# A hybrid decoder layer on one core: another fixed order of the steps where one unit of sparse attention ends and the next begins

## The reference

```python
z = rms_norm(x) @ w_in
# per group of 4 heads that share keys and values
p_cmp = masked_softmax(q . k_cmp);   o_cmp = p_cmp @ v_cmp
imp = sum over the 4 heads of p_cmp @ overlap      # importance of blocks of 64 keys
sel = top_k(imp + forced blocks, 8)
o_slc = softmax(q . k_s over the selected blocks, causal) @ v_s
o_win = softmax(q . k_w over the last 256 keys) @ v_w
o = gate0 * o_cmp + gate1 * o_slc + gate2 * o_win
x = x + concat(retention, short conv, o) @ w_out
x = x + relu(rms_norm(x) @ w_up) ** 2 @ w_down
```

## Time and profile before

| | us |
|---|---|
| median of 3 runs | 3399.78 |
| lowest, highest | 3397.82, 3400.06 |
| the profiled execution, device time | 3393.48 |
| its span, first to last instruction | 3391.7 |
| projection, about | 593 |
| mixers, first to last TensorE instruction | 593 to 1712 |
| output projection and MLP | 1712 to 3392 |

### The profile page before, as it was taken

One profiled execution on the slowest core, in us unless ns is written; L12 is line 12 of the kernel. 1 busy time (PEld: TensorE's weight loads), 2 busy tenths in 40 slices (PEclk: granted clock), 3 DMA queues, 4 the chain that ended last, 5 costly groups with the idle time before them and its releaser, 6 DMA issues. The chain is left out here.

```text
span 3391.7 us, 42938 instructions
## 1 busy us (share of the span) xinstructions
PE 3179.0 (94%) x15498; PEld 2487.8 (73%) x15498; DVE 1443.5 (43%) x2633; ACT 1003.8 (30%) x1660; POOL 1065.3 (31%) x607
## 2 busy tenths in 40 slices
PE   7999998778889999999989699999999999999999
PEld 7999998654555555555458578888888878888887
DVE  3113111456565666665422233345333643354333
ACT  3012000334444444444321132233223222232221
POOL 3212220424232422221010144444444444444442
PEclk9999999678899999999989889999999999999999
DMA  5233221201010100010033332224222332223221
GB/s 175 98 110 100 99 96 63 94 27 65 33 65 33 65 33 33 33 39 7 7 143 134 137 125 94 95 91 149 99 91 95 119 117 98 89 85 124 99 99 62
DMA packets 160807, 289.88 MB, mean 85 GB/s; under 512 B 15023, under 2 KB 122415, under 8 KB 158636
## 3 DMA queue, kind: packets, MB, share of 16 engines
q1 hardware_dynamic: 150908, 270.00, 23.2%
q10 hardware_dynamic: 9776, 18.24, 1.6%
HBM read 237.68 MB, written 50.53 MB: 85 GB/s over the span
## 5 line engine op out<-in xcount | busy, mean ns | idle before, releaser
L1792 POOL TENSOR_TENSOR mlp_down_lo<-mlp_down_raw,mlp_down_hi 128x2048 fp32r<-128x2048 f32 x64 | 298.4, 4663 | 747.7 <-ACT mlp_down_hi L1831 747.7
L1912 DVE TENSOR_TENSOR mlp_y<-mlp_acc,mlp_y 128x512 f32<-128x512 f32 x512 | 344.4, 688 | 198.3 <-PE mlp_acc L1990 194.0
L1990 PE MATMUL mlp_acc<-mlp_down_hi,mlp_f_hi 128*128 128x512 f32 x1024 | 401.2, 392 | 10.5 <-DVE mlp_y L1912 10.5
L1968 PE MATMUL mlp_up<-mlp_hT_hi,mlp_up_hi 128*128 128x512 f32 x1024 | 399.4, 390 | 2.5 <-DVE mlp_hT_lo L1934 2.5
L1990 PE MATMUL mlp_acc<-mlp_down_hi,mlp_f_lo 128*128 128x512 f32 x1024 | 399.3, 390 | 0.0
L1968 PE MATMUL mlp_up<-mlp_hT_hi,mlp_up_lo 128*128 128x512 f32 x1024 | 399.1, 390 | 0.0
L1990 PE MATMUL mlp_acc<-mlp_down_lo,mlp_f_hi 128*128 128x512 f32 x1024 | 399.1, 390 | 0.0
L1968 PE MATMUL mlp_up<-mlp_hT_lo,mlp_up_hi 128*128 128x512 f32 x1024 | 399.1, 390 | 0.0
L1899 DVE TENSOR_TENSOR mlp_f<-mlp_relu 128x512 f32<-128x512 f32 x128 | 134.3, 1050 | 602.1 <-ACT mlp_relu L1838 602.1
L328 PE MATMUL proj_acc<-proj_w_hi,proj_hT_hi 128*128 128x344 f32 x1152 | 370.2, 321 | 10.0 <-issue 9.4
L328 PE MATMUL proj_acc<-proj_w_hi,proj_hT_lo 128*128 128x344 f32 x1152 | 368.3, 320 | 0.0
(11 more groups left out here) (259 smaller groups left out, 5377.6 us busy)
## 6 DMA issues: line engine op xcount, KB each, us to landing
mlp_up_raw<-in_w_up SPq DMA_DIRECT2D x64, 1024.0 KB, 5.2
mlp_down_raw<-in_w_down SPq DMA_DIRECT2D x64, 1024.0 KB, 4.8
proj_w_raw<-in_w_in SPq DMA_DIRECT2D x18, 1376.0 KB, 6.3
z_scratch<-proj_z_out SPq DMA_DIRECT2D x144, 172.0 KB, 1.8
mix_z<-z_scratch SPq DMA_DIRECT2D x16, 1548.0 KB, 6.9
proj_x_tile<-in_x ACTq DMA_DIRECT2D x16, 512.0 KB, 4.0
mixed_scratch<-mix_mixed SPq DMA_DIRECT2D x16, 512.0 KB, 3.0
out_mixed<-mixed_scratch SPq DMA_DIRECT2D x16, 512.0 KB, 4.1
```

The costliest lines, as they stand in the source:

```text
L1792: nc.gpsimd.tensor_tensor(dn_lo[:, b, :, :], dn_raw[:, :, :], dn_hi[:, b, :, :].bitcast(F32), ALU.subtract).then_inc(dn_lo_done, 1)
L1912: nc.vector.tensor_tensor(y[:, yb, tt, cols], acc[i % AR][:, :], y[:, yb, tt, cols], ALU.add).then_inc(added, 1)
L1968: mm = nc.tensor.matmul(up_ps[t % 2][:, :], w[:, b, k, cols], h[:, k, :], start=k == 0 and w is up_hi and h is h_hi, stop=k == KT - 1 and ...
L1990: mm = nc.tensor.matmul(acc[i % AR][:, :], a[:, b, k, tt * P:(tt + 1) * P], w[:, b, k, c * BANK:(c + 1) * BANK], start=k == 0 and a is f_h ...
```

## The change

The rules of `Plan` are rewritten where a unit ends. No instruction is added or dropped, no semaphore and no buffer is changed; the list has the same 2019 steps. Three things are different:

1. The window's lift, turn and post (`front_end`) leave `front`, the selected branch's last values and lift leave `own`, and `row` is split from the selected maxima. They are written out in a head: row, window lift, last values, selected lift, window turn, first scores, window post, selected turn, second scores, select, selected, selected post.
2. What is merged in the body of a unit is shorter by those steps, so the prep pieces, which are spread by count, lie closer together and end earlier; the row stands last in it.
3. The merge is nested in another way: maxima with front and prep first, then own.

```diff
--- before.py
+++ after.py
@@ -468,10 +468,11 @@
 
     def __init__(self, tiles):
         units = tiles * GROUPS
-        first = self.front(0) + self.select(0) + self.front(1) + self.selected_maxima(0)
+        first = self.front(0) + self.front_end(0) + self.select(0) + self.front(1) + self.selected_maxima(0)
         self.steps = self.opening() + merge(first, self.prep(1))
         for u in range(units):
             i, g = divmod(u, GROUPS)
+            last = [("values", u - 1, SLC, (u - 1) // GROUPS), ("lift", u - 1, SLC)] if u >= 1 else []
             own = [("scores", u, SLC, 0)]
             for j in range(1, i + 1):
                 own += [("scores", u, SLC, j), ("values", u, SLC, j - 1)]
@@ -480,17 +481,22 @@
                 pieces = self.prep(i + 2) if i + 2 < tiles else []
                 half = len(pieces) // GROUPS
                 ahead = merge(self.front(u + 2), pieces[g * half:(g + 1) * half])
-
-            self.steps += own[:1]
+            if u + 1 < units:
+                ahead = merge(self.selected_maxima(u + 1)[:-1], ahead) + self.selected_maxima(u + 1)[-1:]
+
+            ends = self.front_end(u + 1) if u + 1 < units else [None, None, None]
+            head = ends[:1] + last + ends[1:2] + own[:1] + ends[2:]
             if u >= 1:
-                self.steps.append(("turn", u - 1, SLC))
+                head.append(("turn", u - 1, SLC))
+            head += own[1:2]
             if u + 1 < units:
-                self.steps += self.select(u + 1)
-                ahead = merge(self.selected_maxima(u + 1), ahead)
+                head += self.select(u + 1)
             if u >= 1:
-                self.steps.append(("post", u - 1, SLC))
-            self.steps += own[1:5] + merge(own[5:] + [("values", u, SLC, i), ("lift", u, SLC)], ahead)
-        self.steps += [("turn", units - 1, SLC), ("post", units - 1, SLC)]
+                head.append(("post", u - 1, SLC))
+            head += own[2:5]
+            self.steps += [step for step in head if step is not None] + merge(own[5:], ahead)
+        self.steps += [("values", units - 1, SLC, tiles - 1), ("lift", units - 1, SLC), ("turn", units - 1, SLC),
+                       ("post", units - 1, SLC)]
 
         self.scores_n = {}
         self.maxima_n = {}
@@ -552,7 +558,12 @@
                   ("scores", u, WIN, window[0])]
         for a, b in zip(window, window[1:]):
             steps += [("scores", u, WIN, b), ("values", u, WIN, a)]
-        return steps + [("values", u, WIN, window[-1]), ("lift", u, WIN), ("turn", u, WIN), ("post", u, WIN)]
+        return steps + [("values", u, WIN, window[-1])]
+
+    @staticmethod
+    def front_end(u):
+
+        return [("lift", u, WIN), ("turn", u, WIN), ("post", u, WIN)]
 
 
 def mixers_phase(nc, z, early, conv_w, q_gain, k_gain, tables, consts, probs, cmp_k, cmp_v, mixed_out):
```

## The result

The changed kernel takes **3414.8 us** (median of 5 runs, 3413.3 to 3418.4), the kernel before in the same session 3397.8 (3395.5 to 3400.1). The ratio is 1.0053, 95% interval 1.0041 to 1.0064: slower by some 17 us, where 20 us less were forecast. Its profiled span is 3411.5 us against 3391.7.

A forecast was written before the change was run, and what follows sets the result against it. TensorE was taken as the bound, its idle time all that an order can win. Ends 30 us, less 14 for the body, plus 4 for the clock: 20 us less, 3380 us for the median, range 3358 to 3396.

The forecast's parts named there:

- The ends: At unit ends in the mixers: of about 56 us lost, 18 and some 8 stay, so 30 us are won.
- The fills of q: In the mixers' body: fills q1 and q0 wait for ScalarE's copies, about 12 and 2 us, costing 14 us.
- the other fills, read by VectorE, and the maxima: In the mixers' body: they move one or two steps either way, costed at nothing, between -3 and +4 us.
- The recorded signs of being wrong: In the mixers: turn waits a microsecond or more, fill q1 waits nowhere, or body's maxima and fill output gain waits.
- The clock: Low-clock stretches near unit ends, 895 to 1290 us: half of five go with the idle time, 4 us won.
- B: At the window's turn: the wait only changes place, 1.1 us for 0.63; 3397; chance 0.16, including near no change.
- C: At the prep bank: a tile's seven fills share it and lose 3 us, break-even 2.3; 3409, slower; chance 0.10.
- A: In the mixers' body: it costs nothing, fills find reads done; 34 us less, 3366 (3361 with all clock); chance 0.20.

The follow-up runs named there:

- e3: The changed kernel with the body merged as in the kernel before in the odd units alone (second half of a tile's prep pieces); 3401.7 us, ratio 1.0030.
- e6: The changed kernel with the normalising of k put behind the compressed branch's post on VectorE again; 3395.3 us, ratio 0.9994.
- e11: The changed kernel with one wait on GpSimd, so the taps' products start only when VectorE has written the tile's packs; 3380.3 us, ratio 0.9962.
- e13: The kernel before with one wait on GpSimd, so the taps' products start only when the tile's packs are written; 3389.6 us, ratio 0.9981.
- e1: The changed kernel's head with the body merged as before, and from tile 4 two values steps behind the last maximum; 3373.2 us, ratio 0.9942.

## Why the prediction was wrong

- **The ends: right in the waits.** Scores for the row's copy went from 24.2 us to nothing, the turn waits 14.3 us in 32 (14 in up to 30 forecast, 0.41 by the bracket), the row 1.9 (under 3 forecast): 29.7 us less by the brackets. That this is worth 30 us of time no run shows by itself.
- **The fills of q: right.** Fill q1 waits 11.3 us in 12 for read q0 (8 to 12 forecast), fill q0 6.9 in 10: the two grew from 4.2 to 18.2, 14.0, the term's own number. Some of that is luck: fill q1 grew by less than its 12 (9.2), fill q0 by more than its 2 (4.8), and e3, which gives the odd units their old spacing back, got only 8 us of time for it.
- **The step that failed** is the price of the rest of the body: the sentence that costs "the other fills, read by VectorE, and the maxima" at nothing, between -3 and +4, and the sum, which has no term for the window's values behind post C or for fill qq behind GpSimd. The wait behind post C grew by 8.8 us, that for `part_max` by 11.6, fill qq's for `keys_zk` by 11.7, fill output's fell by 3.2: +29 in place of 0, seven times the upper bound. With the small ones (-2.2 in sum), the fills of q (14.0), the ends (-29.7) and the clock (+6.6) the account comes to 17.6 us; 17.0 were measured. The recorded signs of being wrong named this one: the body's maxima did gain waits of their own (fill output did not), and the mixers end at 1732 us, not 1692. I walked along TensorE's order and asked of each fill whether its reader was done. I did not walk along VectorE's, where a moved piece goes ahead of another's work, nor ask what runs on GpSimd at the new place. e6 and e11 show that this is what the body paid for: 20 and 31 us come back.
- **It stood in the trace of before.** Two products of one shape, 128x256 with both inputs in SBUF, took 1171 ns (L1127) and 425 ns (L1141). The first stood beside GpSimd's products. Whoever asks why sees that a product's price depends on its place, and that the diff moves four of them.
- **The clock: wrong in sign.** It was to give 4 us. Summed over stretches of 30 us from 900 to 1710, time at the lower level went from 30 to 43 us, and TensorE does half the work there: 6 us lost. These are two profiled executions, and the sum does not follow the time everywhere: e13 has 39 us and is faster than before. Of three new waits two stand right ahead of low stretches (columns as in the earlier trace rows):

```profile
1203.60:1207.00 3.40, 3.40 (x6) 1.35 (x6) 2.00 (x4) 0.00 (x0) 0.00 (x0) 0.50 0.01 2
1271.80:1275.20 3.40, 3.40 (x10) 1.51 (x11) 2.37 (x5) 1.31 (x3) 0.00 (x0) 1.00 0.00 0
1338.80:1342.20 3.40, 3.40 (x6) 1.83 (x7) 2.25 (x4) 0.60 (x1) 0.00 (x0) 0.51 0.00 0
```

  Busy throughout, at half the clock behind the waits of 3.59 us (1203.57) and 2.26 (1338.75), at full behind one of 2.57 (1271.78). More idle time came with more low clock here, but a wait as long as these does not by itself bring it.
- **The rivals.** B falls: the turn's wait is 0.45 us by the bracket and 0.57 from start to start at unit 26, not 1.1. C came out near in size (3409) and wrong in mechanism: the tile's fills of q and qq lost (14.0 + 11.7 - 3.2) / 13 = 1.7 us a tile, below its break-even of 2.3, and fill qq waits for GpSimd's data, not for a read of the shared bank; what tipped the scale was VectorE's queue. A supposed that the body could cost nothing: e1 and e11 show 3373 and 3380 when most of its cost is taken away. Both have new ends and part of the body's waits left. (B's and C's sums leave out the 4 us of the clock that the forecast has.)

## What to carry to other kernels

Before moving a step, walk the queue of every engine that it issues to, not only the bound one's: what it now stands ahead of pays for it, and an engine that is 43% busy can be late at the wait that counts. Look for one shape with two durations in the trace; it may name a neighbour that holds the instruction up, and starting that neighbour later can be worth as much as an order (31 us here, 20 for the swap in the order). When a cured wait brings less than its length, look for the next late thing and mend both at once.

## What the hardware showed

VectorE's products with both inputs in SBUF are held up beside GpSimd's. The product that normalises k took 814 ns in the mean in the changed kernel and 288 where the taps come later (e11). In one tile two of them took 2.71 us (2.72 at worst), about as long as it took GpSimd to end the product it was in and the one behind it:

```profile
780.66 0.78 POOL L911 TENSOR_TENSOR mix_taps<-mix_z 128x256 f32<-128x256 f32 x1
...
780.79 2.71 DVE L1149 TENSOR_TENSOR mix_kn<-mix_z,mix_rstd 128x128 f32<-128x128 f32 x2
...
781.52 1.82 POOL L912 TENSOR_TENSOR mix_taps<-mix_taps,keys_conv_taps 128x768 f32<-128x768 f32 x1
```

The reciprocal, one input, took 1753 ns in the mean with the products beside it as without them. Not every instruction with one input goes free: the scaling ahead of it (L1136, 128x256) took 0.28 or 0.29 us in 15 tiles and 0.82 in one, at 1071.18, where a product of GpSimd (L911) was already running. GpSimd paid next to nothing: its product of 128x768 took 1827 ns in the changed kernel and 1854 in e11.

```profile
L912 POOL TENSOR_TENSOR mix_taps<-mix_taps,keys_conv_taps 128x768 f32<-128x768 f32 x16 | 29.2, 1827 | 1.3
```

```profile
L913 POOL TENSOR_TENSOR mix_taps<-mix_taps,keys_conv_taps 128x768 f32<-128x768 f32 x16 | 29.7, 1854 | 1.3
```

The Trainium skill (SBUF — State Buffer, section Who interferes with whom) says that a VectorE instruction with two SBUF inputs contends with a GpSimd instruction that reads SBUF, and that the one issued later is blocked until the other ends. The trace agrees for the products with two inputs, 814 ns against 288, and with the reciprocal, which is free; the scaling with one input that once took 0.82 us shows that two inputs are not the whole of it. That nearly all of the price fell on VectorE here is the trace's to say; the page has either one pay.
